# Projection stage of a decoder step: when token tile 1 is asked for, turned and projected, beside the first two products of token tile 0

## The reference, cut to what matters

```python
m = (jax.nn.silu(c) @ w_mod_l + b_mod_l).reshape(B, 6, 1, D)
sh1, sc1, g1, sh2, sc2, g2 = [m[:, i] for i in range(6)]
mix_out, new_state = mix_fn(x * (1 + sc1) + sh1)
# inside mix_fn:
p, u, v, q, kv, gates = split_proj(h @ lp['w_in'])      # w_in is 1024 x 2072
vn = layer_norm(v, lp['sgu_ln_g'], lp['sgu_ln_b'])
```

## Time and profile before

| what | value |
|---|---|
| time, median of 3 runs | 1429.99 us (1428.22 to 1431.51) |
| the profiled execution | 1433.1 us |
| its span, first to last instruction | 1431.0 us |
| PE busy | 1241.3 us, 87% |
| DVE busy | 723.6 us, 51% |
| ACT busy | 542.5 us, 38% |
| POOL busy | 111.2 us, 8% |
| mean granted TensorE clock | 0.925 |

### The profile page before, as it was taken

The page is one execution under the profiler, slowest core; times in us unless marked ns, Lnnn a source line. Parts: engine busy times, 40 slices in busy tenths (PEclk is TensorE's granted clock), DMA queues, the critical chain, the costliest instruction groups (busy, mean ns, idle before and its releaser), DMA issues. The chain is left out here.

```text
span 1431.0 us, 21333 instructions
## 1 busy us (share of the span) xinstructions
PE 1241.3 (87%) x7878; PEld 903.9 (63%) x7879; DVE 723.6 (51%) x1452; ACT 542.5 (38%) x910; POOL 111.2 (8%) x167
## 2 busy tenths in 40 slices
PE   3299999999957999999998997289999999999862
PEld 1156666666546656666666885267788887788730
DVE  0012221222233455666666765788658568685148
ACT  0000000000022667656554221276546466564132
POOL 1000001100000000000000000001001011010050
PEclk9599999999956899999999998599999999999986
DMA  9843334400054522000004332699769669894582
GB/s 321 270 150 135 129 128 136 72 23 13 10 166 151 204 77 43 1 1 2 1 2 157 118 118 81 237 373 361 270 236 354 250 240 376 302 319 163 200 301 95
DMA packets 89697, 235.57 MB, mean 165 GB/s; under 512 B 7450, under 2 KB 15061, under 8 KB 89463
## 3 DMA queue, kind: packets, MB, share of 16 engines
q1 hardware_dynamic: 76711, 192.19, 39.0%
q0 software_dynamic: 8144, 27.62, 5.3%
q10 hardware_dynamic: 4768, 14.75, 2.7%
HBM read 196.49 MB, written 40.13 MB: 165 GB/s over the span
## 5 line engine op out<-in xcount | busy, mean ns | idle before, releaser
L2188 PE MATMUL psum<-w_hi,x_parts 128*128 128x512 f32 x736 | 239.0, 396 | 10.6 <-DVE x_parts L2307 9.8
L2300 DVE TENSOR_TENSOR w_lo<-raw,w_hi 128x2048 fp32r<-128x2048 f32 x96 | 215.6, 2287 | 58.1 <-ACT w_hi L2247 58.0
L2247 ACT CAST w_hi<-raw 128x2048 fp32r<-128x2048 f32 x96 | 178.6, 1914 | 83.1 <-DVE work L2318 51.2
L595 PE MATMUL psum<-low,high 128*128 128x512 f32 (+5 forms) x576 | 200.6, 502 | 0.0
L2188 PEld LDWEIGHTS psum<-w_hi,x_parts 128*128 128x128 f32 x736 | 138.9, 189 | 42.3 <-issue 13.6
L595 PEld LDWEIGHTS psum<-low,high 128*128 128x128 f32 (+1 forms) x576 | 105.4, 188 | 77.9 <-issue 67.2
L2188 PE MATMUL psum<-w_lo,x_parts 128*128 128x512 f32 x368 | 143.9, 391 | 0.0
L1496 DVE CUSTOM_DVE_ANT_0 low<-psum,high 128x512 f32<-128x512 f32 (+5 forms) x172 | 93.2, 579 | 78.1 <-PE psum L1197 67.0
L2188 PE MATMUL psum<-w_hi,a_parts 128*128 x368 | 120.5, 399 | 5.9 <-DVE a_parts L2313 5.9
L1409 ACT ACTIVATE low<-low,high 128x640 f32<-128x640 f32 (+9 forms) x140 | 98.8, 708 | 44.5 <-DVE high L1496 44.1
L1227 PE MATMUL psum<-keep,low 128*128 128x128 f32 (+1 forms) x556 | 103.5, 293 | 11.5 <-ACT high L1420 4.8
(11 more groups left out here) (317 smaller groups left out, 1437.9 us busy)
## 6 DMA issues: line engine op xcount, KB each, us to landing
raw<-in_moe_w_gate SPq DMA_DIRECT2D x16, 2048.0 KB, 11.2
raw<-in_moe_w_up SPq DMA_DIRECT2D x16, 2048.0 KB
raw<-in_moe_w_down SPq DMA_DIRECT2D x16, 2048.0 KB, 11.4
high<-in_w_mod SPq DMA_DIRECT2D x12, 2048.0 KB, 13.9
y_d<-work ACTq DMA_DIRECT2D x24, 512.0 KB, 7.0
high<-in_x_prompt SPq DMA_DIRECT2D x16, 512.0 KB, 3.9
y_d<-high SPq DMA_DIRECT2D x1, 8192.0 KB, 23.6
low<-in_w_in SPq DMA_DIRECT2D x3, 2048.0 KB, 15.6
```

Of the source, the lines that this page charges most:

```text
L595: mm = pe.matmul(c.bank(2 + n % 2)[0:T, 0:w], hT[i % 2][:, k, 0:T], c.w_in[:, k, a:a + w], start=(k == 0), stop=(k == KT - 1))
L2188: mm = pe.matmul(out, left[l][:, k * P:(k + 1) * P], w[:, bass.ds(at + k * step, 512)], start=n == 0, stop=n == len(steps) - 1)
L2247: act.copy(c.w_hi[:, at:at + PART // 2], c.raw[:, o:o + PART // 2]).then_inc(hi_done[p], 1)
L2300: dve.tensor_tensor(c.w_lo[:, at:at + PART // 2], c.raw[:, o:o + PART // 2], c.w_hi[:, at:at + PART // 2].bitcast(F32), ALU.subtract).then ...
```

## The change

On SP, tile 1 is asked for behind the third piece of `w_in` (`load_w(2)`) and not behind the fifth; tile 2 is asked for ahead of halves 4 and 5 of `w_mod`, right behind the write of the bias table. On TensorE, in the round of tile 0, `transposes(1)` moves from the head of the round to behind `sample_gate_weights`, so that `chunk(0, 0)`, `chunk(0, 1)`, the bias table and the gate weights come before it. On ACT, `h_part(1)` moves behind the two copies of `chunk(0, 0)`; on DVE, it moves behind `table_and_gate_weights`. In tile 0, DVE waits for the six small transfers before it uses the norm's weights (before the change, TensorE alone waited for them, in `pool_window(0)`). The rounds of tiles 1 to 8 keep their order.

```diff
             load_w(2)
+            load_x(1)
             load_w(3)
...
             load_w(4)
...
-            load_x(1)
             sp.wait_ge(tab_done, 1)
             sp.dma_start(c.tab_d, tab[0:NH, :].unsqueeze(1).to_broadcast([NH, TROWS, TABW])).then_inc(c.tab_out, 16)
+            load_x(2)
             mod_load(c, sp, 4)
             mod_load(c, sp, 5)
-            load_x(2)
...
@@ block.tensor
-                if i + 1 < NT:
+                if 1 <= i < smp:
                     transposes(i + 1)
                 if i < NT:
                     chunk(i, 0)
...
                     sample_gate_weights()
+                    transposes(1)
@@ block.scalar
-                if i + 1 < smp:
+                if 1 <= i < smp - 1:
                     h_part(i + 1)
                 act.wait_ge(z_ready, 4 * i + 1)
...
                 act.copy(zuv[s][0:T, 0, :], c.bank(2)[0:T, PW:2 * PW]).then_inc(z_act, 1)
+                if i == 0:
+                    h_part(1)
@@ block.vector
+                if i == 0:
+                    table_and_gate_weights()
                 if i + 1 < NT:
                     h_part(i + 1)
-                if i == 0:
-                    table_and_gate_weights()
...
+                    if i == 0:
+                        dve.wait_ge(small_in, 16 * 6)
                     linked(dve.tensor_tensor(vn, vn, c.lnv_g[0:Ti, :], ALU.mult))
```

More of the change, by code:

```diff
@@ L420, in load_w, with load_x @@
                 sp.dma_start(c.w_in[:, :, a:a + w], w_src[:, :, a:a + w]).then_inc(c.w_in_in[n], 16)
+            def load_x(i):
+                sp.wait_ge(xT_ready, i)
+                T = tile_rows(i)
+                src = t["x_prompt"][0, i * P:(i + 1) * P, :] if i < smp else t["x_sample"].rearrange("b j d -> (b j) d")
+                sp.dma_start(x[0:T, :], src).then_inc(c.x_in, 16)
             load_w(0)
@@ L440, in _ @@
             load_w(4)
[L441 to L445, removed]
             def load_bias(a):
```

## The result

The changed kernel takes 1398.67 us (median of 4 runs, 1394.94 to 1402.17), against 1430.75 us for the kernel before on the same occasion: ratio 0.9764, 95% interval 0.9739 to 0.979. Forecast were 1403.0 us with a range of 1399.5 to 1410.0 us.

A forecast was written before the change was run, and what follows sets the result against it. TensorE, idle until tile 1 lands, was taken to bound the start: first product 40.6 us, plus 18.7, 22.03 and 0.93 us, turns tile 2 at 82.3 us instead of 109.28, saving 27.0 us: median 1403.0 us, range 1399.5 to 1410.0 us.

The forecast's parts named there:

- What bounds the kernel: TensorE idle from 40.46 to 65.03 us for tile 1; the turning of tile 2, at 109.28 us, sets all later rounds.
- Start of the first product: Tile 0's first product need not wait for tile 1 and starts at about 40.6 us, not 66.80 us.
- The low stretch at the start: Tile 0's first product starts cold: 6.4 us at clock 0.50, a loss of 3.2 us.
- The rest of tile 0: Sample gate weights to queries' end: 22.03 us, a low stretch of 6.90 us included, plus 0.93 us for turning tile 1.
- the first rival: Clock holds through the 2.30 us wait for VectorE; tile 2 sets the start at 79.4 us: 1400.1 us, chance 0.13.
- Tile 1's covers: Tile 1 lands at about 54.8 us, at worst 65.0 us, piece 4 at 65.0 us; turning at about 60.4 us.
- Tile 2 behind the bias table's write: On the queue, write and tile take 14.4 us from 65.0 us; tile 2 lands at 79.4 us, 2.9 us early.
- One low stretch less: Clock holds through the 2.30 us wait for VectorE; 29.9 us saved, 1400.1 us, chance 0.13.
- Late tile 2: Tile 2, behind the bias table's write, lands after 82.3 us, up to 90.6 us: 1405.5 to 1411.3 us, chance 0.14.
- no effect of the queue: Tile 1 still lands at 65.0 us, so its turning waits 4.6 us: 1407.6 us, chance 0.03.
- given back later: A later stage waits for something unmoved, or its low stretches fall otherwise: 1405 to 1412 us, chance 0.04.
- slow all through: Clock stays at 1.2 GHz through tile 0's TensorE work: 1429.1 us, up to 1465 us, chance 0.02.

The follow-up runs named there:

- fill_wait: Changed kernel plus eight unread turns of the identity on TensorE in front of its wait for VectorE's masked gate weights: 1398.56 us.
- cover_wait: Changed kernel with tile 1's turning and tile 0's third product moved ahead of the sample gate weights, into the wait for VectorE: 1399.28 us.
- tile1_late: Changed kernel with tile 1 asked for behind piece 4 of `w_in` again, as before the change: 1406.34 us.
- products_alone: Changed kernel with both places on the queue put back, so only the order of the engines is changed: 1406.66 us.
- after_third: The changed kernel run again with no edit, in the third group: 1397.71 us.
- after_again: The changed kernel run again with no edit, in the first group: 1400.07 us.
- fill_whole: Changed kernel plus 20 unread turns of the identity on TensorE in front of its wait for VectorE's masked gate weights: 1394.82 us.
- split: As cover_wait, but VectorE copies product 1 out before it waits for the sample gate weights: 1393.77 us.
- split_x2: As split, with tile 2 also asked for ahead of the bias table's write: 1393.73 us.
- tile2_behind: Changed kernel with tile 2 asked for behind halves 4 and 5 of `w_mod` again, as before the change: 1407.11 us.

## Why the prediction was right or wrong, point by point

**What bounds the kernel.** Right. The idle TensorE ahead of tile 1 was the loss, the later rounds kept their length (36.04 us in both), and what was saved before tile 2 stayed saved.

**Start of the first product.** Forecast 40.6 us, measured 39.91, 39.97 and 39.88 us. The last half of the modulation landed a little earlier; 0.7 us. Not foreseen: in four kernels (fill_wait, cover_wait, tile1_late, products_alone) the modulation was done still earlier and the product waited for piece 0 of `w_in`, as in fill_wait:

```profile
PE psum L598 <- DMA low<-in_w_in: 3.0, 1, 3.0
```

It then started at 38.4 to 38.9 us. In the profiles of kernels with the new order of the engines, tile 0's modulated form and piece 0 are ready within 2.3 us of each other, now the one first and now the other, so moving either alone further ahead should bring little; no run here tried it.

**The low stretch at the start: the step that failed.** "In the changed kernel the start is cold too. I take a low stretch between the two that the rows have, 5.85 and 6.90 us." Neither row stands behind what this product stands behind: the first follows 24.5 us of idle TensorE, the second the pause among the tables. In the changed kernel the engine has just done the last half of the modulation and the turning of tile 0, and pauses 1.7 us. Nor did the product start a low stretch of its own. The clock had already fallen at about 32.7 us in the changed kernel's profile and 32.5 us in after_third, while TensorE did the last half of the modulation, and what the product met was the tail; in after_again the clock had fallen at about 32.0 us and was back by 35.5 us. The stretch from 36 to 40 us, in the changed kernel and in after_again:

```profile
36.00:40.00 4.00, 2.29 (x11) 1.92 (x10) 1.60 (x5) 1.50 (x4) 1.40 (x3) 0.50 1.09 344
```

```profile
36.00:40.00 4.00, 1.64 (x13) 1.19 (x12) 2.17 (x7) 1.50 (x4) 1.96 (x4) 1.00 1.09 366
```

So the length of that tail hangs on when the clock fell, and neither of the two rows could give it. The variants show the same: in tile1_late, products_alone, fill_wait, fill_whole and cover_wait the clock was at 1.00 when the product began, fell at 39.6 to 39.9 us and stayed low for 3.4 us. What decides when it falls stays open. The low stretch was 3.05, 0 and 2.9 us, its cost 1.5, 0 and 1.5 us where I had 3.2 us. The range of the forecast allowed each of the two stretches only 1 us more or less, half a microsecond of time. The work at full clock, 15.54 us, was right to 0.1 us (15.63 us in after_again). From first product to sample gate weights this makes 17.1, 15.6 and 17.1 us for 18.7 us forecast.

**The rest of tile 0.** 22.96 us forecast; 22.6, 21.2 and 22.6 us measured. The second low stretch was there in all three, as the row said, in full length twice and once about half as long. That it hangs on the pause was my reading too, in the first rival; fill_whole bears it out.

The earlier start and these two together are why tile 2 is turned at 79.58, 76.68 and 79.44 us and not at 82.3 us: 2.7 to 5.6 us.

For the profiled execution the sum closes. From the forecast 1403.0 us to the measured 1398.67 us there are 4.3 us: 0.7 us from the start of the first product, 1.6 us from the first low stretch, 0.4 us from the rest of tile 0, 1.1 us from what follows the turning of tile 2 (1320.6 us for 1321.7 us) and 0.4 us because this execution lies 3.5 us over the median of its runs where I took 3.1 us; the last 0.1 us is rounding. The low stretch is the largest of the terms, and twice the 0.8 us by which the time lies below the range. The last two are scatter.

**Tile 1's covers.** Right. Tile 1 landed 15.1 us behind its issue at 38.23 us, at 53.3 us (54.8 us forecast), ahead of its turning at 58.2 us; piece 4 at 52.85 + 11.6 = 64.5 us, ahead of the queries. The rows of the changed kernel, issue and landing:

```profile
38.23 3.62 SPq L426 DMA_DIRECT2D high<-in_x_prompt  x1
...
high<-in_x_prompt SPq DMA_DIRECT2D x1, 512.0 KB, 15.1
...
low<-in_w_in SPq DMA_DIRECT2D x1, 2048.0 KB, 11.6
```

**Tile 2 behind the bias table's write.** Forecast to land at 79.4 us, it landed at 60.21 + 12.7 = 72.9 us:

```profile
60.21 0.36 SPq L426 DMA_DIRECT2D high<-in_x_prompt  x1
...
high<-in_x_prompt SPq DMA_DIRECT2D x1, 512.0 KB, 12.7
```

The write was over-sized: I let its data wait for piece 4 to drain and then charged it in full. Tile 2 came 8.4 us behind piece 4, where 14.4 us were forecast; the write had been issued at 56.36 us, 8.1 us before piece 4 landed, so it had time to move part of its data beside it. The write has no landing in the profile that would show this. The pair split and split_x2 puts what the write holds tile 2 back at about 7 us, where I had charged 14.4 us less tile 2's own 1.6 us, 12.8 us. The rule of the Trainium skill on ring order ("DMA: Bandwidth & Descriptors", "Queues, rings and completion order"), which I had cited for the danger, is borne out in so far as tile 2 did land later behind the write than ahead of it; it cost no time. The error had no price, since TensorE came at 79.58 us; but it hid that there was room for the faster cases, because I let tile 2 stop the first rival at 79.4 us.

**The rivals.** "One low stretch less" at 1400.1 us was nearest in time, and not what happened: the first stretch was short or missing and not the second. The rule of the Trainium skill that I set beside it ("TensorE: Matmul & The Clock Gate", "Why this matters for your kernels") asks for no long idle gaps between bursts and so lets short ones pass. It is not borne out here: 2.30 us, and in fill_wait 1.27 us, were followed by 0.50. It is borne out by the 2.88 to 3.18 us ahead of tile 2 in the four profiles of before, which left 1.00. Late tile 2, no effect of the queue, given back later and slow all through did not occur; tile2_behind and tile1_late are the first two brought about by an edit, and cost 7.0 and 6.3 us.

**The range.** Its lower end was the first rival's. A case with both stretches short was never priced: 39.9 + 15.6 + 19.5, the full-clock lengths of after_again and fill_whole, is 75.0 us, 34 us before 109.28 us, and some 1396 us. The trace of before had a hint that a cold start was not certain: while tile 0 was modulated there, the clock was 1.00. But it fell at about 40.1 us, with TensorE idle, just ahead of the 40.6 us at which I had the product start, so the hint was a weak one. A stretch of the kernel before:

```profile
39.00:40.00 1.00, 0.00 (x0) 0.00 (x0) 1.00 (x4) 1.00 (x3) 0.13 (x1) 1.00 1.11 368
```

**The base.** One profiled execution carried the sum. I set it 3.1 us over the median of the three runs that I had; over the median of 1430.75 us of the later occasion it is 2.4 us. Its tile 2, at 109.28 us, was turned 1.6 to 2.1 us later than in the three other profiles of before. Against the four profiles of before, whose tile 2 is at 107.8 us on average, the changed kernel's three (78.6 us) save 29.3 us; the times say 31 to 32 us. The 2 to 3 us between are within the scatter of the rest, and are not explained further.

## What to carry to other kernels

When work is moved to the head of a stage, do not take the clock it will start at from how the same work started in the old order. Look at what its engine does before it in the new one, and at where the low stretches of those rows begin and end; and since two executions of one kernel differ here, price the case without a low stretch too. Two late transfers in a row are worth the longer of the two waits, not their sum: take both places back together before crediting each. And a pause can be paid twice, once as idle time and again at the low clock, as the 1.3 to 2.3 us among the tables were here; the longer pause behind the queries was not, so read the clock in the row behind it first. Taking a wait out helps only if it does not come back one engine further on, as it did in cover_wait.

## What the runs showed of the hardware

The changed kernel began its first product at a granted clock of 0.50 for 2.9 to 3.05 us (two profiles) or not at all (one), and the stretch behind its 2.30 us pause was low for about 3.4 us (after_again) or about 6.8 us (the two others). In the kernel before, a pause of 2.88 to 3.18 us behind the queries left the clock at 1.00 in all four profiles, where the 2.30 us among the tables brought about 6.8 us at 0.50. The time from the turning of tile 2 on differed by 8.6 us between four profiles of the kernel before (1313.1 to 1321.7 us). A 576 KB write to memory, issued some 7 to 8 us before the 2 MB transfer in front of it had landed, made the 512 KB behind it land 8.4 and 8.5 us after that transfer (the changed kernel and split), where they landed 1.2 us after it when asked for ahead of the write (split_x2).
